# Last expert tile added by TensorE straight from SBUF, and the pair rows loaded earlier: a two-layer hybrid decoder step on one core

## The reference

```python
def hier_moe(h, ...):
    # top-1 group of 4, top-2 of the 8 experts in it, weights normalised
    combine = ...                      # (tokens, 32), two entries not zero per token
    out = 0
    for e in range(32):
        hid = silu(h @ w_gate[e]) * (h @ w_up[e])     # 1024 -> 256
        out = out + combine[:, e:e+1] * (hid @ w_down[e])  # 256 -> 1024
    return out

x = x + hier_moe(rms_norm(x))          # both layers
y = rms_norm(x)                        # after layer 1
```

## Time and profile before

| what | value |
|---|---|
| median of 3 runs | 1039.96 us (1038.82 to 1040.89) |
| profiled execution | 1040.27 us |
| its span in the profile | 1038.5 us |
| TensorE matmul busy | 906.1 us, 87% of the span |
| VectorE, ScalarE, GpSimd busy | 40%, 28%, 28% |
| DMA | 277.71 MB, 415 to 420 GB/s in the middle of each expert stage |
| mean granted TensorE clock | 0.947 of full speed |

### The profile page before, as it was taken

One profiled execution on the slowest core, in us unless ns is written; L12 is line 12 of the kernel. 1 busy time (PEld: TensorE's weight loads), 2 busy tenths in 40 slices (PEclk: granted clock), 3 DMA queues, 4 the chain that ended last, 5 costly groups with the idle time before them and its releaser, 6 DMA issues. The chain is left out here.

```text
span 1038.5 us, 18756 instructions
## 1 busy us (share of the span) xinstructions
PE 906.1 (87%) x7250; PEld 658.1 (63%) x7250; DVE 414.2 (40%) x955; ACT 287.7 (28%) x595; POOL 293.3 (28%) x438
## 2 busy tenths in 40 slices
PE   7999999974999889875799999989849998887885
PEld 6988888963555555542687878579745555545553
DVE  5366784255111111111768878773552111111114
ACT  6356673131111111110532112362302111111103
POOL 1810000013343343211052527720123443443110
PEclk9999999996999999999589999999969999999997
DMA  7612111777999999996824636315869999999966
GB/s 234 187 36 52 51 42 54 272 300 295 373 416 416 417 413 415 418 420 237 266 67 127 159 85 159 92 50 220 359 256 362 414 415 418 416 415 419 420 277 254
DMA packets 112277, 277.71 MB, mean 267 GB/s; under 512 B 34952, under 2 KB 73176, under 8 KB 88074
## 3 DMA queue, kind: packets, MB, share of 16 engines
q1 hardware_dynamic: 96630, 253.74, 64.2%
q0 software_dynamic: 11424, 17.87, 4.7%
q10 hardware_dynamic: 4132, 4.86, 1.9%
HBM read 266.25 MB, written 27.45 MB: 283 GB/s over the span
## 5 line engine op out<-in xcount | busy, mean ns | idle before, releaser
L2106 DVE COPY areaB<-ps 128x512 f32<-128x512 f32 x66 | 45.6, 691 | 344.7 <-PE ps L2089 344.7
L2072 PE MATMUL ps<-ring,areaB 128*64 128x256 f32 x576 | 139.4, 397 | 24.6 <-issue 20.5
L2073 PE MATMUL ps<-ring,areaB 128*64 128x256 f32 x576 | 139.8, 398 | 0.0
L2118 POOL DMA_INDIRECT pair_rows<-areaB,idx x66 | 67.7, 1026 | 246.5 <-DVE areaB L2106 238.4
L2072 PEld LDWEIGHTS ps<-ring,areaB 128*64 128x64 f32 x576 | 79.0, 142 | 64.8 <-issue 25.2
L2097 ACT ACTIVATE v_rows<-ps 128x256 f32<-128x256 f32 x66 | 25.3, 384 | 256.5 <-PE ps L2073 256.5
L1058 PE MATMUL ps<-conv_x_high,pw_halves 128*128 128x272 f32 x512 | 90.1, 297 | 1.8 <-DVE areaS L1293 1.8
L2113 POOL DMA_INDIRECT areaC<-h_rows,idx x66 | 68.8, 1042 | 64.2 <-issue 45.8
L2094 ACT ACTIVATE areaB<-ps 128x512 f32<-128x512 f32 x66 | 39.4, 597 | 156.4 <-PE ps L2062 156.4
L2073 PEld LDWEIGHTS ps<-ring,areaB 128*64 128x64 f32 x576 | 79.0, 143 | 0.0
L2089 PE MATMUL ps<-ring,areaB 128*64 128x512 f32 x320 | 76.1, 593 | 2.7 <-DVE areaB L2103 1.6
(11 more groups left out here) (379 smaller groups left out, 1893.9 us busy)
## 6 DMA issues: line engine op xcount, KB each, us to landing
ring<-in_w_down SPq DMA_DIRECT2D x40, 1024.0 KB, 23.9
ring<-in_w_gate SPq DMA_DIRECT2D x32, 1024.0 KB, 23.7
ring<-in_w_up SPq DMA_DIRECT2D x32, 1024.0 KB, 26.4
wring<-in_w_down SPq DMA_DIRECT2D x12, 1024.0 KB, 25.7
areaS<-in_w_down SPq DMA_DIRECT2D x12, 1024.0 KB
wring<-in_w_pw SPq DMA_DIRECT2D x24, 512.0 KB, 4.6
areaA<-in_w_gate SPq DMA_DIRECT2D x10, 1024.0 KB, 27.1
areaA<-in_w_up SPq DMA_DIRECT2D x10, 1024.0 KB, 29.3
```

Of the source, the lines that this page charges most:

```text
L2072: pe.matmul(ps[0:CAP, 2 + odd, 0:F], rows, ring_gate(ws)[:, k, :], start=(k == 0), stop=(k == KT - 1))
L2073: mm = pe.matmul(ps[CAP:P, 2 + odd, 0:F], rows, ring_up(ws)[:, k, :], start=(k == 0), stop=(k == KT - 1))
L2106: return v.tensor_copy(rows_out[:, s, :], ps[:, 5 + odd, :])
L2118: return gp.indirect_dma_start(pair_half_rows, bass.IndirectOffsetOnAxis(idx[:, RING + s:RING + 1 + s], 0), rows_out[:, s, :], None, bound ...
```

## The change

The last tile's rows no longer go through DRAM. They stay in `rows_out`, and TensorE adds them to the tokens by a matmul with `late_T`, a matrix (slot by token) that holds the token's weight where its choice sits in that slot. VectorE builds it in `weigh_late` behind tile 10 (20 steps) and takes those weights out of `weight`; TensorE turns it behind tiles 12 and 14, ScalarE copies it behind tiles 13 and 15. `pair_rows` is filled with token rows in the attention stage, so that places that the last tile leaves open hold finite numbers.

SP loads the pairs when tile 31 is multiplied and its rows are stored (`early_rows_stored`), into ring places that are free by then. In the last step TensorE multiplies down of tile 31 ahead of gate and up of tile 32. In layer 0 the turned pair sums come by matmuls with the identity in place of transposes, into the banks that hold the late product. In layer 1 two `turn_x` run ahead of the last gate and up, four of the five token tiles are scaled and mixed as in layer 0 (`mix`), and the diagonal matmul stays for the last alone.

The core of the diff:

```diff
@@ attention_stage, sync
                     for i in range(6, NW):
                         sp.wait_ge(w_ready[i % 2], i // 2)
                         load_weights(sp, i)
+                        if i < 10:
+                            c, a = (i - 6) // 2, (i - 6) % 2
+                            sp.dma_start(pair_rows[c * T + a * NP // 2:c * T + (a + 1) * NP // 2, :],
+                                         x_prompt2[a * NP // 2:(a + 1) * NP // 2, :]).then_inc(pairs_filled, 16)
+                            if a:
+                                sp.dma_start(pair_rows[c * T + NP:(c + 1) * T, :], x_sample2).then_inc(pairs_filled, 16)
@@ to_stream, tensor
                 def tensor(self, pe):
-                    pe.wait_ge(out_kept, NCH)
-                    for i, t in enumerate(ORDER):
+                    def late(i):
+                        t = ORDER[i]
                         r = rows_of(t)
-                        pe.wait_ge(mixed, i + 1)
                         if i >= 4:
                             pe.wait_ge(added, i - 3)
                         for k in range(KT):
-                            mm = pe.transpose(banks(i)[:, k // 4, (k % 4) * P:(k % 4) * P + r],
-                                              x_rows[0:r, t, k * P:(k + 1) * P], ident[0:r, 0:r])
+                            at = slice(k // 4 * CAP, (k // 4 + 1) * CAP)
+                            pe.matmul(banks(i)[:, k // 4, (k % 4) * P:(k % 4) * P + r], late_rows[at, (k % 4) * P:(k % 4 + 1) * P],
+                                      late_T[at, t * P:t * P + r], start=(k % 4 == 0), stop=False)
+
+                    def turn(i):
+                        t = ORDER[i]
+                        r = rows_of(t)
+                        pe.wait_ge(mixed, i + 1)
+                        for k in range(KT):
+                            mm = pe.matmul(banks(i)[:, k // 4, (k % 4) * P:(k % 4) * P + r],
+                                           pair(t)[0:r, 0, k * P:(k + 1) * P], ident[0:r, 0:r], start=False, stop=(k % 4 == 3))
                         mm.then_inc(turned, 1)
+
+                    pe.wait_ge(late_kept, 2)
+                    pe.wait_ge(out_kept, NCH)
+                    for i in range(4):
+                        late(i)
+                    turn(0)
+                    turn(1)
+                    late(4)
+                    for i in range(2, NT):
+                        turn(i)
@@ to_outputs
+                def before_last(self, pe):
+                    self.turn_x(pe, 1)
+                    pe.wait_ge(out_kept, NCH - 1)
+                    self.turn_x(pe, 0)
+
                 def tensor(self, pe):
...
+                        if i >= 2:
+                            self.turn_x(pe, i)
+                        for c in range(2):
+                            at = slice(c * CAP, (c + 1) * CAP)
+                            mm = pe.matmul(banks(i)[0:r, c, :], late_T[at, t * P:t * P + r], late_rows[at, :], start=False, stop=i < NT - 1)
...
                 def vector(self, v):
+                    def mix(i):
+                        t = ORDER[i]
+                        r = rows_of(t)
+                        v.wait_ge(first_scaled, i + 1)
+                        v.scalar_tensor_tensor(pair(t)[0:r, 0, :], pair(t)[0:r, 1, :], weight[0:r, NT + t:NT + t + 1],
+                                               pair(t)[0:r, 0, :], ALU.mult, ALU.add).then_inc(mixed, 1)
...
-                    for t in ORDER:
-                        v.tensor_scalar(diag[:, t, :], ident[:, :], weight[:, t:t + 1], None, ALU.mult).then_inc(diag_ready, 1)
+                    v.tensor_scalar(diag, ident[:, :], weight[:, ORDER[-1]:ORDER[-1] + 1], None, ALU.mult).then_inc(diag_ready, 1)
                     v.wait_ge(final_gain_landed, 16)
+                    mix(0)
+                    mix(1)
                     add_up(0)
-                    for i in range(1, NT):
-                        add_up(i)
-                        finish(i - 1)
+                    mix(2)
+                    add_up(1)
+                    finish(0)
+                    mix(3)
+                    add_up(2)
+                    finish(1)
+                    add_up(3)
+                    finish(2)
+                    add_up(4)
+                    finish(3)
                     finish(NT - 1)
@@ expert_stage, sync
                         next_down(e, this)
+                    sp.wait_ge(down_done, last)
+                    sp.wait_ge(early_rows_stored, 1)
+                    load_pairs(sp, l)
                     if l == 1:
                         sp.dma_start(final_gain, final_norm_g.rearrange("(a n) -> a n", a=1).to_broadcast([P, D])).then_inc(final_gain_landed, 16)
                     more.sync(sp, spill_of(sp))
-                    sp.wait_ge(rows_complete, 1)
-                    load_pairs(sp, l)
                     combine.sync(sp)
@@ expert_stage, gpsimd
-                        store(Tile(e))
-                    spilled = spill_of(gp)
+                        if e < last:
+                            store(Tile(e))
                     for s in range(RROW):
-                        gp.wait_ge(scattered[s], 16 * len(range(s, NCH, RROW)))
-                    more.gpsimd(gp, spilled)
-                    gp.sem_inc(rows_complete, 1)
+                        gp.wait_ge(scattered[s], 16 * len(range(s, last, RROW)))
+                    gp.sem_inc(early_rows_stored, 1)
+                    more.gpsimd(gp, spill_of(gp))
@@ expert_stage, tensor, step
+                        if x.e in LATE_PE:
+                            turn_late(pe, (range(4), (4,))[LATE_PE.index(x.e)]).then_inc(late_turned, 1)
+                        if final:
+                            out(x.shift(-1))
+                            combine.before_last(pe)
                         pe.wait_ge(turned_kept, x.e + 1)
...
-                        gate_and_up(pe, x.s, x.odd, x.gs, last_half_landed if final else None).then_inc(gateup_done, 1)
+                        gate_and_up(pe, x.s, gateup_bank(x), x.gs, last_half_landed if final else None).then_inc(gateup_done, 1)
                         if first:
                             table_matmuls(pe, next_match, 0, next_table, 7)
-                        else:
+                        elif not final:
                             out(x.shift(-1))
@@ expert_stage, vector
+                        if x.e == LATE_DVE:
+                            weigh_late()
+
+                    def weigh_late():
+                        n = Steps(v, late_step)
+                        is_late, late_weight = fullest_hot, rank_next
+                        twice = match.rearrange("p (t a) s -> p t a s", a=2)
+                        n.link(v.tensor_scalar(is_late, expert_no, order[:, NE - 1:NE], None, ALU.is_equal))
+                        for c in range(2):
+                            n.link(v.tensor_tensor(hot, picked[c], is_late.unsqueeze(1).to_broadcast([P, NT, NE]), ALU.mult))
+                            n.link(v.tensor_reduce(late_weight[:, c * NT:(c + 1) * NT], hot, AX_X, ALU.add))
+                        n.link(v.scalar_tensor_tensor(late_weight, rank, float(CAP), late_weight, ALU.is_lt, ALU.mult))
+                        n.link(v.tensor_tensor(late_weight, late_weight, weight, ALU.mult))
+                        n.done(v.tensor_tensor(weight, weight, late_weight, ALU.subtract))
+                        for c in range(2 * NT):
+                            n.done(v.tensor_scalar(twice[:, c % NT, c // NT, :], slot_no[:, :], rank[:, c:c + 1], late_weight[:, c:c + 1],
+                                                   ALU.is_equal, ALU.mult))
+                        n.wait()
+                        n.link(v.tensor_tensor(twice[:, :, 0, :], twice[:, :, 0, :], twice[:, :, 1, :], ALU.add))
+                        n.done(v.tensor_copy(twice[:, :, 1, :], twice[:, :, 0, :]))
```

More of the change, by code:

```diff
@@ L1966, in sync, with turn_x @@
                         sp.wait_ge(y_ready, i + 1)
-                        sp.dma_start(dst, pairs[0:r, t, 1, :]).then_inc(y_stored, 16)
+                        sp.dma_start(dst, pair(t)[0:r, 1, :]).then_inc(y_stored, 16)
                     sp.wait_ge(y_stored, 16 * NT)
-                def tensor(self, pe):
-                    def turn_x(i):
+                def turn_x(self, pe, i):
+                    t = ORDER[i]
+                    r = rows_of(t)
+                    for k in range(KT):
+                        pe.matmul(banks(i)[0:r, k // 4, (k % 4) * P:(k % 4 + 1) * P],
+                                  x_T[:, k, t * P:t * P + r], ident[:, :], start=(k % 4 == 0), stop=False)
@@ L1972, in turn_x, with scalar, scale_first @@
+                def scalar(self, act):
+                    def scale_first(i):
                         t = ORDER[i]
                         r = rows_of(t)
-                        for k in range(KT):
-                            pe.matmul(banks(i)[0:r, k // 4, (k % 4) * P:(k % 4 + 1) * P],
```

(21 more changed lines are left out.)

132 lines of the change are left out of this document (93 added, 39 removed).

## The result

The changed kernel takes 1051.12 us (median of 4 runs, 1049.37 to 1053.3) against 1039.39 (4 runs, 1038.63 to 1040.89): ratio 1.0116, 95% interval 1.0093 to 1.014, or 9.7 to 14.6 us more. I had forecast 1047.3. The sign and the main mechanism are as forecast; the amount was 3.8 us too small. The profiled execution took 1049.67 with a span of 1047.9, which is 9.4 above the span of before.

A forecast was written before the change was run, and what follows sets the result against it. Expert stages were taken as bound by the weight stream, with the tail behind it counting. Layer 0's +0.8 and layer 1's +6.5 gave +7.3, span 1045.8, plus 1.8 less 0.3: 1047.3 us, range 1042.5 to 1051.5.

The forecast's parts named there:

- The gain behind the pair loads: End of layer 1, largest term: final_gain lands 13.9 us after the pair loads begin, upper bound 15.1, holding all VectorE mixes.
- VectorE from there: End of layer 1, after the gain lands: mixes, sums and finishes take 18.5 us, then the last store 3.06.
- Layer 1 in sum: End of layer 1: 1045.0 against 1038.5, +6.5 us; +4.9 if the clock does not fall.
- The clock at the last tile: TensorE, both layers: gaps of 4.6 and 5.6 us halve the clock; out(31) takes 3.5 us instead of 1.94.
- Rival 1: TensorE's clock holds through both gaps: -1.9 and +4.9, together +3.0, 1043.0 us; chance 0.13.
- Layer 0: End of layer 0: TensorE's late and turn work takes 16.8 us, last add +1.4; +0.8 after the conv stage's gain.
- The rule of the Trainium skill that I had set aside: Turns in layer 0: transpose mode four times faster for fp32, so a full identity-matmul turn takes 4.7, layer 0 another +11.
- The conv stage's warm start: Conv stage's first 6 us, at 0.50 before, could run warm: 0 to 1.2 us back, 0.6 taken.
- What I costed at nothing: weigh_late, transposes and small copies at tiles 10 to 15, and six fill copies in attention: hidden, no cost.
- The sum: Whole kernel: +0.8 in layer 0 and +6.5 in layer 1, +7.3 on the span, 1047.3 us.
- Rival 2: End of layer 1: gain lands in time beside the pair rows; 1040.9, no change, or 1036.1 with clock held; chance 0.12.
- Rival 3: Slower: half-rate late work (+3), gain at state_conv's pace (+1.2), or tile 10's 2 us uncovered; 1050 to 1052; chance 0.13.

The follow-up runs named there:

- the old order: Changed kernel with gate and up of tile 32 again ahead of tile 31's down product, gain still loaded behind the pairs: 1046.12 us, ratio 1.0074.
- fillers: Changed kernel plus five unread 512-column identity matmuls in TensorE's wait ahead of tile 31's down product, both layers: 1046.74 us, ratio 1.0068.
- the first pair of profiles: First profiled executions of the kernel before and of the changed kernel: tail 0 34.88 and 37.13 us, tail 1 38.84 and 46.58.
- the second profile of after: Changed kernel run once more, unchanged: 1050.85 us, ratio 1.0116; its profile has tails of 37.07 and 47.05.
- The fill copies: Kernel before plus only the six copies into pair_rows in the attention stage and the wait for them: 1038.74 us, ratio 1.0000.
- the building of the matrix: Kernel before plus only building the late matrix, which nothing reads, weights left whole: 1038.76 us, ratio 0.9993.
- the old four: Four profiles with the old instructions in both tails: two of the kernel before, one with fill copies, one with the late matrix; mean tails 34.6 and 38.85 us.
- the first repair: Changed kernel with the gain's load back straight behind the last down weights: 1043.52 us, ratio 1.0049.
- both repairs: Changed kernel with the gain's load back at its old place and TensorE's old order at the last tile: 1038.98 us, ratio 1.0008.

## Why the prediction was right, and where it was mis-sized

**The gain behind the pair loads: mechanism right, size too small.** I had the load land 13.9 us after the first pair load; it took 15.8 (1026.50 less 1010.68), and 16.0 and 16.1 in the profiles with the old order and with fillers. The forecast's upper bound of 15.1 was too low as well. Its 13.9 added 1.3 us for 0.5 MB to a landing of the last pair at 12.6. The pace was not what failed. Windows of after:

```profile
1013.68:1024.68 11.00, 8.94 (x51) 4.42 (x47) 1.17 (x3) 4.02 (x5) 0.00 (x0) 1.00 1.02 408
1024.68:1026.50 1.82, 1.82 (x14) 1.17 (x12) 0.00 (x0) 0.00 (x0) 0.00 (x0) 1.00 0.08 34
```

The 16 engines moved 408 GB/s, and 14.0 us after the first pair load (1024.68) the 4.98 MB were all but through, where the forecast had the landing. Then 1.8 us passed with the engines at a share of 0.08 before VectorE's wait ended. The sum had nothing between the last bytes and the landing; that stretch is the term it lacked. `state_conv`, from which I had the upper bound, was the nearer guide. (The prediction names 370 GB/s beside its 12.6, but that number comes out only with about the 0.41 MB/us that it uses for the gain; with 0.37 it is 13.9 for the pairs alone.) Issuing the five pair loads took 3.27 us, where it took 2.41 before, and the gain was issued 3.31 behind the first of them; but that is not the reason, since with the old order it was issued 2.84 behind and landed 16.0 after.

**VectorE from there: right.** Forecast 18.5 us, measured 18.34 (1026.50 to 1044.84), with waits of 0.49 and 0.16 for ScalarE where I had put 0.6 and 0.2. The last store took 3.06.

**Layer 1 in sum.** Forecast +6.5, measured +7.7 in the first pair of profiles and +8.0 between the means (46.8 less 38.85). Measured from the copy of tile 30, which came 1.66 later in after than in before (998.26 against 996.60, a difference that arose upstream), the pair loads came 0.5 earlier than forecast, the gain landed 1.9 later behind them, and VectorE took 0.2 less: +1.2.

**The clock at the last tile: right.** Forecast 3.5 us for `out(31)` at half rate, measured 3.68 and 3.42, with TensorE idle 4.44 and 4.58 before it; the fillers (1.94) show that the clock is the cause. The 3.5 us at half rate that the prediction gave the fall had no row behind it. In after the clock stood at 0.50 until about 1006.3 in layer 1, 3.0 us behind the product's start, and until about 484.0 in layer 0, 5.4 us behind it. Rival 1 is out.

**Layer 0: sign right, size too small.** Forecast +1.4 for the tail, measured +2.25, and +2.5 between the means (37.1 less 34.6). From the start of tile 31's product, where the forecast began its count (479.34), it is +3.4 in the first pair of profiles and +3.5 between the means. The late work began 12.5 us behind that start (491.19 less 478.65), forecast 12.2. The late and turn work was forecast at 16.8 and took 18.5 (491.19 to 509.68), and its terms were wrong in both directions: the four late products together took 4.84 and not 6.55, but `turn(0)` and `turn(1)` took 5.54 and not 2.85, since the clock fell again to 0.50 at 498, which I had only in the range. That the turns "wait for nothing longer" failed too: the last one waited 0.72, because the mix of its pair stood on VectorE behind a sum that had waited for TensorE:

```profile
505.16 1.23 DVE L1970 TENSOR_TENSOR x_T<-ps,x_T 128x1024 f32<-128x1024 f32 x1 [1.20 <-PE ps L1943]
506.30 1.28 DVE L1962 SCALAR_TENSOR_TENSOR ring<-ring,areaS 128x1024 f32<-128x1024 f32 x1
```

The last pair also came later than forecast, without setting the end here: it was scaled 16.55 us after the loads began, not 13.6. The loads began 2.5 us earlier than before and ended no earlier (502.99; 502.46 in the earlier trace rows). The queue moved 324 GB/s meanwhile:

```profile
486.50:503.00 16.50, 14.45 (x124) 12.29 (x122) 6.53 (x8) 5.27 (x7) 0.00 (x0) 0.90 0.97 324
```

That is 5.35 MB for 4.46 MB of pair rows, and in before it was 351 GB/s over 488.9 to 502.5, 4.77 MB. So 0.6 MB more of other data came in ahead of the last pair. It is no accident of one profile: every profile with the changed kernel's loads has the last pair scaled 16.4 to 17.5 us after the first load, and the four with the old loads 13.5 to 13.9. That the data is `state_conv` and the conv weights, which SP issues right behind, was not tested, and their being there is not enough: the kernel before issues them too, `state_conv` 2.5 us behind its first pair load where it is 3.2 in after. What in the changed loads does it stays open. The last of the windows shown at the end (500 to 502) has the 16 engines fully busy, 1.01, at only 202 GB/s.

The rule of the Trainium skill that I had set aside ("TensorE: Matmul & The Clock Gate", Terms) stays contradicted: a full tile's turn by identity matmuls took 2.05 us, not 4.7.

**The conv stage's warm start: seen in the clock, not in the time.** It does start at 1.00 instead of 0.50. I gave it 0.6 us, and the first pair of profiles seemed to give 1.07 (487.32 against 488.39). But the middle varies from 486.5 to 488.4 among kernels with the old tails, and the second profile of after has 488.15: nothing can be read from it.

**What I costed at nothing: right.** The fill copies 1.0000 (0.9983 to 1.0018), the building of the matrix 0.9993 (0.9978 to 1.0008).

**The sum.** By the means the tails grew 2.5 and 8.0, 10.5 us, where the medians say +11.7, with 9.7 to 14.6 in the interval. The tails explain the result within its uncertainty. If the weight stream sets when tile 31's product starts, as its wait says, layer 0 is to be counted from there: +3.5, and with layer 1's 8.0 it is 11.5. The wait that this leaves out was 1.0 us shorter in the changed kernel (4.8 against 5.9 in the mean of the old four); whether the change or the stream shortened it, no run shows. The forecast had +7.3. Of the 4.4 that it lacks, counted so, 1.5 are layer 1 (8.0 against 6.5), 2.1 layer 0 (3.5 against 1.4), 0.6 the warm start that did not show, and 0.2 are without a place. Against the absolute 1047.3 the miss is 3.8, since the runs of before came out 0.6 lower this time.

**Rival 2**, the gain in time, is what the first repair makes true by hand; it gave back 7.3. **Rival 3** named a landing at the pace of `state_conv` and half-rate late work as ways to 1050 to 1052. The landing came (later still), half rate caught `turn(0)` and `turn(1)` alone, and that is where the time fell. Its third part, the uncovered 2 us at tile 10, did not.

## What to carry to other kernels

Before a load is moved on a queue, find every wait for it and what stands behind that wait: here a 0.5 MB constant, needed late, held all of VectorE's work for 7.8 us, and either an early load or a wait placed at its first use took most of that away. When a burst of work on TensorE is moved out of a gap, the gap can cost twice, as it did here: the idle time (4.4 to 4.6 us) and the half rate behind it (3.4 to 3.7 us for a product of 1.94). Filler matmuls proved that, and keeping the old order gave the same within these runs (1046.1 and 1046.7, tails within 0.6 us). Work moved from a busy engine to another pays only if its operands are there in time; here it held up what stood behind it in the queue. And a stretch that is compared between kernels has to start at an event that the bound itself sets: tail 0 started one event too early, and with both repairs it showed a gain of 1.0 us where there was a loss of 1.0.

## What the runs showed of the hardware that I had not expected

- TensorE's granted clock fell to 1.2 GHz while it was busy without a gap. Windows of after:

```profile
492.00:494.00 2.00, 2.00 (x35) 2.00 (x35) 0.94 (x2) 1.15 (x1) 0.00 (x0) 1.00 1.02 403
494.00:496.00 2.00, 2.00 (x29) 1.88 (x26) 0.56 (x1) 0.00 (x0) 0.00 (x0) 1.00 1.02 406
496.00:498.00 2.00, 2.00 (x18) 1.94 (x17) 0.00 (x0) 1.15 (x1) 0.00 (x0) 0.92 1.03 414
498.00:500.00 2.00, 2.00 (x10) 2.00 (x10) 1.62 (x2) 1.15 (x1) 0.00 (x0) 0.50 1.07 351
500.00:502.00 2.00, 2.00 (x15) 1.88 (x14) 0.47 (x1) 0.00 (x0) 0.00 (x0) 0.72 1.01 202
```

  The work before the fall was the late product on 64 rows and `turn(0)` on 32 rows. The second profile of the changed kernel shows the same two us later, and the one with fillers has 0.54 over 496 to 498. No run separates the shape of these matmuls from what came before them.
- Late products whose operands alternate between the two halves of the rows ran 16 in 1.23 us instead of 1.71, and 64 in 3.84 instead of 4.84.
- The same kernel reaches the copy of tile 30 in layer 0 at 473.3 or at 476.3 us (two profiles of before), and the range is 472.5 to 479.2 among all profiles. In the two of before the difference is there ahead of the expert stage already: GpSimd's first gather starts at 240.95 and at 244.18.
